# Up projections of two MLPs by one level of Strassen's method: seven quarter products per block

## The reference

```python
def sq_relu_mlp(h, w_up, w_down):
    return jnp.square(jax.nn.relu(h @ w_up)) @ w_down
```

## Time and profile before

| | us |
|---|---|
| median of three runs | 1588.3 (1588.07 to 1589.31) |
| the profiled execution, its own time | 1586.16 |
| its span in the profile | 1584.4 |
| first up unit of layer 0 starts | 500.8 |
| up 2 to up 15 with down 0 to 11, layer 0 | 526.5 to 887.0 |
| down 12 and 13, layer 0 | 887.0 to 914.2 |
| down 12 begins, layer 1 | 1513.4 |

### The profile page before, as it was taken

The page is one execution under the profiler, slowest core; times in us unless marked ns, Lnnn a source line. Parts: engine busy times, 40 slices in busy tenths (PEclk is TensorE's granted clock), DMA queues, the critical chain, the costliest instruction groups (busy, mean ns, idle before and its releaser), DMA issues.

```text
span 1584.4 us, 22657 instructions
## 1 busy us (share of the span) xinstructions
PE 1499.1 (95%) x9438; PEld 1334.8 (84%) x9438; DVE 865.4 (55%) x1298; ACT 502.2 (32%) x835; POOL 74.7 (5%) x119
## 2 busy tenths in 40 slices
PE   4899999988899999999999999989999999999995
PEld 3799999755688988998998879768899899889984
DVE  2693455677457644434334685935673433444378
ACT  2333333266516322222222244242632222222220
POOL 1200000010101000000000010000100000000002
PEclk8999999999999999999999999999999999999998
DMA  9421232475741322122222221461132222221211
GB/s 316 134 80 54 80 108 94 137 227 190 244 142 54 105 82 80 58 76 80 79 79 80 80 71 63 150 204 54 54 109 78 80 80 81 80 79 56 76 54 67
DMA packets 127770, 162.27 MB, mean 102 GB/s; under 512 B 3314, under 2 KB 103018, under 8 KB 127682
## 3 DMA queue, kind: packets, MB, share of 16 engines
q1 hardware_dynamic: 123106, 146.57, 28.6%
q0 software_dynamic: 3760, 11.80, 2.6%
q10 hardware_dynamic: 816, 2.65, 0.4%
HBM read 157.34 MB, written 3.67 MB: 102 GB/s over the span
## 4 chain that ended last, share of the span: by engine, by line
PE 86%; DVE 8%; ACT 2%; DMA 2%; issue 1%; POOL 0%; SPq 0%; ACTq 0%; DVEq 0%; POOLq 0%
PE ps L588 39%; PE ps L570 30%; PE ps L579 5%; PE ps L621 2%; PE ps L820 1%; PE ps L917 1%; DVE wlo L1544 1%; PE ps L797 1%; PE ps L940 1%; DMA raw<-in_w_mod_l 1%; PE ps L635 1%; DVE ln_small L1992 1%; PE ps L928 1%; ACT whi L1147 1%; DMA vec_rows<-in_b_mod_l 1%
## 5 line engine op out<-in xcount | busy, mean ns | idle before, releaser
L1147 ACT ACTIVATE whi<-raw 128x2048 fp32r<-128x2048 f32 x88 | 168.1, 1912 | 358.4 <-PE ps L588 353.4
L570 PE MATMUL ps<-h_hi,whi 128*128 128x320 f32 x1088 | 251.4, 313 | 12.3 <-DVE wlo L1544 7.7
L570 PE MATMUL ps<-h_lo,whi 128*128 128x320 f32 x1088 | 250.6, 312 | 0.0
L570 PE MATMUL ps<-h_hi,wlo 128*128 128x320 f32 x1088 | 250.3, 312 | 0.0
L588 PE MATMUL ps<-whi,hid_hi 128*128 128x512 f32 x640 | 249.4, 390 | 0.0
L588 PE MATMUL ps<-wlo,hid_hi 128*128 128x512 f32 x640 | 249.1, 389 | 0.0
L588 PE MATMUL ps<-whi,hid_lo 128*128 128x512 f32 x640 | 249.0, 389 | 0.0
L1544 DVE TENSOR_TENSOR wlo<-raw,whi 128x2048 fp32r<-128x2048 f32 x88 | 201.5, 2291 | 70.8 <-ACT whi L1147 66.7
L570 PEld LDWEIGHTS ps<-h_hi,whi 128*128 128x128 f32 x1088 | 184.7, 190 | 15.9 <-issue 11.8
L570 PEld LDWEIGHTS ps<-h_lo,whi 128*128 128x128 f32 x1088 | 184.4, 190 | 0.0
L570 PEld LDWEIGHTS ps<-h_hi,wlo 128*128 128x128 f32 x1088 | 184.4, 190 | 0.0
(11 more groups left out here) (269 smaller groups left out, 1871.8 us busy)
## 6 DMA issues: line engine op xcount, KB each, us to landing
raw<-in_w_mod_l SPq DMA_DIRECT2D x43, 1024.0 KB, 5.2
raw<-in_w_up_l SPq DMA_DIRECT2D x32, 1024.0 KB, 5.5
raw<-in_w_down_l SPq DMA_DIRECT2D x32, 1024.0 KB, 5.0
raw<-in_w_in_l SPq DMA_DIRECT2D x15, 1024.0 KB, 5.2
raw<-in_w_out_l SPq DMA_DIRECT2D x8, 1024.0 KB, 5.1
raw_more<-in_w_mod_l SPq DMA_DIRECT2D x5, 1024.0 KB, 9.8
out<-x_tok SPq DMA_DIRECT2D x5, 512.0 KB, 2.6
x_tok<-in_x_sample ACTq DMA_DIRECT2D x4, 512.0 KB, 6.8
```

The lines of the kernel that those rows point to most:

```text
L570: mm = pe.matmul(outs[hf], w_of(still, k), a_of(part, k, hf), start=(k == 0 and part == 0 and still == 0), stop=(k == nk - 1 and still == 1))
L1147: act.activation(whi[:, w % 2, :], raw_block(k), ACT.Copy).then_inc(hi_done, 1)
```

## The change

From up block 2 on, a block (1024 x 256 weights, 640 tokens) is cut into four weight quarters and four token quarters, and its product is made from seven quarter products of 12 matmuls each (Winograd's form), in place of eight. GpSimd forms the three weight sums that need it (`weight_sums`: four `tensor_tensor` instructions of 128 x 512; one sum is written over a raw quarter). The splits of a block become six pieces with seven quarters (3584 elements in place of 2048). VectorE forms the four sums of token quarters once per layer (`token_sums`), and puts seven products together with seven additions from PSUM (`combine`), two `squared` and two `low_u` in each block. The high and low parts of the token sums take the place of `x` (`thi` at the address of `x_tok`) and of unused quarters of `h`; the full-precision `h` (`hf32`) lies where `acc` is. So `x` is stored to memory by GpSimd's queue before the MLP (`spill_x`) and fetched back when up 15 has ended (`fetch_normed`), together with the norm's gain and bias; tiles 0 and 1 are then rescaled on VectorE, tiles 2 to 4 on GpSimd (`scale_x`), and all ten `gated_sum` come behind down 13. Down blocks are split in two pieces. The two gate vectors change places, and the mixer's gated output goes through the small buffer `pg`.

```diff
+        hf32 = at("h_full", 148, [P, KT, TOK])
+        thi = at("t_hi", 48, [P, KT, TOK], F32R)
+        tlo = at("t_lo", 176, [P, 2, 4, HALF], F32R)
+        sb = at("w_sums", 186, [P, 3, 512])
+        tf = tmp[:].rearrange("p a n -> p (a n)")
+        quad = [[tf[:, TOK * (1 + n):TOK * (2 + n)], tf[:, 0:TOK]] for n in range(2)]
...
+        NPROD, NCOMB = 7, 7
+        PAR = [w % 2 for w in W_UP]
+        PIECES = ((0,), (1, 2), (3,), (4,), (5,), (6,))
+        LN_X = (0, 2, 2 + NT, 4 + NT)
...
+            def spill_x(layer):
+                for t in range(NT):
+                    pool.wait_ge(ln_n, 2 * NT * layer + t + 1)
+                    pool.dma_start(A["x_spill"][t * P:(t + 1) * P, :], x[:, t, :]).then_inc(x_re, 16)
+            def weight_sums(layer, u, i=None):
...
+                r = raw_block(w_k[w]).rearrange("p (k n) -> p k n", n=BW)
+                a11, a12, a21, a22 = r[:, 0:4, 0:P], r[:, 4:8, 0:P], r[:, 0:4, P:BW], r[:, 4:8, P:BW]
+                s2, s1, s4 = (sb[:, n, :].rearrange("p (k n) -> p k n", n=P) for n in range(3))
+                raw_ready(pool, w_k[w], i)
+                if u > 2:
+                    before = w - 1 if strassen(w - 1) else w - 3
+                    pool.wait_ge(lo_done, lin(OPS[before] + 2, PER, i))
+                pool.tensor_tensor(s1, a21, a22, ALU.add).then_inc(sums, 1)
+                pool.wait_ge(sums, lin(c + 1, 16, i))
+                pool.tensor_tensor(s2, s1, a11, ALU.subtract).then_inc(sums, 1)
+                pool.tensor_tensor(a21, a11, a21, ALU.subtract).then_inc(sums, 1)
+                if u > 2:
+                    pool.wait_ge(lo_done, lin(OPS[before] + 5, PER, i))
+                pool.wait_ge(sums, lin(c + 2, 16, i))
+                pool.tensor_tensor(s4, a12, s2, ALU.subtract).then_inc(sums, 1)
+            def fetch_normed(layer):
+                pool.wait_ge(up_mm[layer], 4 + 14 * NPROD)
+                pool.wait_ge(x_re, 16 * NT * (2 * layer + 2))
+                for t in range(NT):
+                    pool.dma_start(x[:, t, :], A["x_spill"][t * P:(t + 1) * P, :]).then_inc(x_re, 16)
+                load_gb(2 * layer)
+            def scale_x(layer):
+                pool.wait_ge(x_re, 16 * NT * (2 * layer + 3))
+                pool.wait_ge(gb_ld, 32 * (2 * layer + 1))
+                for t in range(2, NT):
+                    pool.tensor_tensor(x[:, t, :], x[:, t, :], gb[:, 0, :], ALU.mult).then_inc(x_g, 1)
+                    pool.wait_ge(x_g, 6 * layer + 2 * t - 3)
+                    pool.tensor_tensor(x[:, t, :], x[:, t, :], gb[:, 1, :], ALU.add).then_inc(x_g, 1)
+                pool.wait_ge(x_g, 6 * layer + 6)
+            def mlp(layer):
+                spill_x(layer)
+                for n in (2, 3):
+                    weight_sums(layer, n)
+                for kind, n, i in mlp_steps(pool):
+                    if kind == "up" and n > 3:
+                        weight_sums(layer, n, i)
+                fetch_normed(layer)
+                scale_x(layer)
+                load_gb(2 * layer + 1)
...
+            T1, T2 = t_part(0, 0, tlo[:, 1]), t_part(4, 1, tlo[:, 0])
+            T3, T4 = t_part(0, 1, hhi[:, 0:4, HALF:TOK]), t_part(4, 0, hlo[:, 0:4, HALF:TOK])
+            PRODUCTS = ((0, h_part(0, 0)), (1, T2), (2, T1), (3, T3), (0, h_part(4, 0)), (1, h_part(4, 1)), (2, T4))
             def up(layer, u, i=None):
                 w = w_ord[S.index(("up", layer, u))]
+                c = NCOMB * (14 * layer + u - 2)
+                for item, (b, moving) in enumerate(PRODUCTS):
+                    for g, its in enumerate(PIECES):
+                        if item == its[0]:
+                            pe.wait_ge(lo_done, lin(OPS[w] + g + 1, PER, i))
+                    if u == 2 and item == 0:
+                        pe.wait_ge(relu_h0[layer], 4 * (layer + 1))
+                    seen = (c - 2, c - 1, c, None, None, c + 1, c + 2)[item]
+                    if seen is not None and (u > 2 or item >= 5):
+                        pe.wait_ge(comb, lin(seen, 4 * NCOMB, i))
+                    if item == 4:
+                        pe.wait_ge(first_out, lin(14 * layer + u - 1, 4, i))
+                    if u == 2 and item in (1, 2, 3, 6):
+                        pe.wait_ge(t_lo, 4 * layer + (1, 2, 3, 4)[(1, 2, 3, 6).index(item)])
+                    product(b, w, item, moving).then_inc(up_mm[layer], 1)
...
+            def high_t(layer, n, k0, hf):
+                if n == 0:
+                    act.wait_ge(x_re, 16 * NT * (2 * layer + 2))
+                act.wait_ge(t_sum, 4 * layer + (3, 3, 3, 4)[n])
+                cols = slice(hf * HALF, (hf + 1) * HALF)
+                act.activation(thi[:, k0:k0 + 4, cols], hf32[:, k0:k0 + 4, cols], ACT.Copy).then_inc(t_hi, 1)
+            def first_quad(layer, u, i=None):
+                act.wait_ge(up_mm[layer], lin(4 + NPROD * (u - 2) + 1, 4 * NPROD, i))
+                if u > 3:
+                    act.wait_ge(sq_lo[layer], lin(2 * u - 3, 8, i))
+                act.activation(quad[u % 2][0][:, 0:HALF], bank(0, 0, HALF), ACT.Copy).then_inc(first_out, 1)
...
             def mlp(layer):
                 for n, (f, hf) in enumerate(FIRST):
                     first_relu(layer, f, hf)
+                    if n == 3:
+                        high_t(layer, 0, 4, 1)
+                        high_t(layer, 1, 0, 0)
+                    if n == 4:
+                        high_t(layer, 2, 0, 1)
+                        high_t(layer, 3, 4, 0)
                     if n == 5:
-                        split_hi(W_UP[layer] + 2)
+                        split_hi(W_UP[layer] + 2, None, (0, 1, 2))
+                late = True
                 for kind, n, i in mlp_steps(act):
                     w = w_ord[S.index((kind, layer, n))]
+                    if kind == "down":
+                        split_hi(w + 1, i, (0, 1, 2) if strassen(w + 1) else None)
+                        late = True
+                        continue
+                    if late:
+                        split_hi(w, i, (3, 4, 5))
+                        late = False
+                    first_quad(layer, n, i)
+                    if strassen(w + 1):
+                        split_hi(w + 1, i, (0, 1, 2, 3, 4))
+                        high_u(layer, n, 0, i)
+                        split_hi(w + 1, i, (5,))
+                    else:
+                        split_hi(w + 1, i)
+                        high_u(layer, n, 0, i)
+                    high_u(layer, n, 1, i)
                 split_hi(w_ord[S.index(("down", layer, 15))])
...
-                mark(dve.tensor_tensor(acc[:, t, cols], acc[:, t, cols], gate[:, 1, int(t == LAT), cols], ALU.mult))
+                if t >= 2:
+                    dve.wait_ge(x_g, 6 * layer + 2 * t - 2)
+                else:
+                    dve.wait_ge(ln_x, LN_X[2 * layer] + t + 1)
+                mark(dve.tensor_tensor(acc[:, t, cols], acc[:, t, cols], gate[:, 0, int(t == LAT), cols], ALU.mult))
...
+            def token_sums(layer):
+                def quarter(k0, hf):
+                    return hf32[:, k0:k0 + 4, hf * HALF:(hf + 1) * HALF]
+                b11, b12, b21, b22 = quarter(0, 0), quarter(0, 1), quarter(4, 0), quarter(4, 1)
+                dve.wait_ge(ln_lo, NT * 2 * layer + NT)
+                dve.tensor_tensor(b11, b12, b11, ALU.subtract).then_inc(t_sum, 1)
+                dve.wait_ge(t_sum, 4 * layer + 1)
+                dve.tensor_tensor(b12, b22, b12, ALU.subtract).then_inc(t_sum, 1)
+                dve.wait_ge(t_sum, 4 * layer + 2)
+                dve.tensor_tensor(b22, b22, b11, ALU.subtract).then_inc(t_sum, 1)
+                dve.wait_ge(t_sum, 4 * layer + 3)
+                dve.tensor_tensor(b21, b21, b22, ALU.subtract).then_inc(t_sum, 1)
+            def low_t(layer, n, k0, hf, dst):
+                dve.wait_ge(t_hi, 4 * layer + n + 1)
+                if n == 2:
+                    dve.wait_ge(up_mm[layer], 4)
+                cols = slice(hf * HALF, (hf + 1) * HALF)
+                dve.tensor_tensor(dst, hf32[:, k0:k0 + 4, cols], thi[:, k0:k0 + 4, cols].bitcast(F32),
+                                  ALU.subtract).then_inc(t_lo, 1)
+            def combine(dst, a, b, layer, prods, seen, i):
+                dve.wait_ge(up_mm[layer], lin(prods, 4 * NPROD, i))
+                if seen:
+                    dve.wait_ge(comb, lin(seen, 4 * NCOMB, i))
+                dve.tensor_tensor(dst, a, bank(b, 0, HALF), ALU.add).then_inc(comb, 1)
...
+            def squared(dst, src):
+                return dve.scalar_tensor_tensor(dst, src, 0.0, src, ALU.max, ALU.mult)
+            def up_step(layer, u, i, late):
...
+                q11, q12 = (quad[u % 2][0][:, n * HALF:(n + 1) * HALF] for n in range(2))
+                q21, q22 = (quad[u % 2][1][:, n * HALF:(n + 1) * HALF] for n in range(2))
+                if late:
+                    split_lo(w, i, (3, 4, 5))
+                if two_ups:
```

(124 more changed lines are left out.)

163 lines of the change are left out of this document (80 added, 83 removed).

## The result

The changed kernel takes 1601.4 us (median; 1601.1 to 1602.2) where the kernel before, run beside it, takes 1588.5: ratio 1.0082, with a 95% interval of 1.0064 to 1.0099. It is 0.8% slower. I had forecast 1573.0 and a range of 1561 to 1600. The profiled execution took 1601.32 us, its span is 1598.9.

A forecast was written before the change was run, and what follows sets the result against it. The prediction took TensorE's matmul issue to bound the MLPs. Saved matmuls -49.3 us, waits at the ends +23.2, clock +4, starts +6.8 gave -15.3 us: 1573.0 us, range 1561 to 1600.

The forecast's parts named there:

- I let one of its 2.1 us instructions in first: End of an MLP, before down 14's split: one GpSimd instruction delays VectorE; TensorE loses 0.6 us in down 13.
- I add one of them, 1.1 us: Start of an MLP: GpSimd's weight sums meet crowded VectorE work, and one sum's 1.1 us is added.
- GpSimd blocks VectorE: Rival, both MLP ends and starts: GpSimd and VectorE instructions alternate; +7.5 us in all, 1595.8 us; chance 0.30.
- Steady state: Up and down block pairs: an up block takes 12.32 us in place of 14.08, VectorE's lag costs zero.
- the rival of the VectorE-bound pair: Up blocks: longer VectorE steps lose 1.5 us a pair, 21 us over 14 pairs, 1594 us; chance 0.10.
- Start without interference: Start of an MLP: VectorE's token sums and low parts make TensorE late by 2.3 us, before any GpSimd sum.
- End without interference: End of an MLP: TensorE 11.6 us late at down 15's split in each layer, plus 2 us of clock.
- The clock: After TensorE's stand at an MLP's end the granted clock must recover: 2 us a layer.
- GpSimd's prices: GpSimd's two-operand instructions, weight sums and rescales: 1.1 us for 512 elements, 2.1 us for 1024.
- U + 15: End of an MLP: the fetch of `x`, gain and bias lands 15 us after up 15 ends (U).
- the late trip through memory: Rival, end of an MLP: the fetch lands 20 us after up 15 ends, giving 1581 us; chance 0.08.

The follow-up runs named there:

- Run 1: The change with GpSimd's gain and bias for token tiles 2 to 4 cut to one column: 1580.0 us, 0.9945 of the kernel before.
- run 2: The change with only one element of each GpSimd weight sum formed, the rest left out: 1591.2 us, 1.0017 of the kernel before.
- run 5: The change with both GpSimd's rescale of tiles 2 to 4 and its weight sums made tiny: 1565.2 us, 0.9868 of the kernel before.
- run 6: The change with the stores of `x` issued between GpSimd's shares of the norm, not together: 1601.3 us, 1.0089 of the kernel before.
- run 3: The change with all rescales on VectorE, tiles 2 to 4 in a row behind down 13's groups: 1594.4 us, 1.0034 of the kernel before.
- run 9: The change with the end spread on VectorE, stores between norm shares, and `low_t` 2 and 3 ahead of the last two first lows: 1570.6 us, 0.9890.
- run 10: As run 9, and GpSimd waits with up 3's weight sums until the low parts of the token sums are done: 1571.3 us, 0.9894.
- run 11: Spread end, stores between norm shares; last two first lows behind up 2's fourth `combine`, up 3's sums behind up 2's fifth split: 1569.6 us, 0.9888.
- run 4: The change with the split of down 15 moved ahead of the ten gated sums: 1600.5 us, 1.0081 of the kernel before.
- run 7: The change with all rescales on VectorE, an earlier fetch, and gate and rescale spread between groups at the MLP's end: 1571.9 us, 0.9888.

## Why the prediction was wrong

**The step that failed** is, at the end of an MLP, "I let one of its 2.1 us instructions in first". I gave GpSimd one hold for the whole stretch; the trace shows five before the split of down 14 is done, 2.1 us each. From them came the second wait of TensorE, 9.4 and 9.2 us, for which the forecast had 0.6. Run 1 shortens GpSimd's instructions there and gives 21 us back. At the start it is the same step, "I add one of them, 1.1 us": the trace shows six between `h_lo` at 507.23 and the last first low at 533.14, 1.0 to 1.1 us each, 6.2 in all. The price of a hold was right at both places, their number was not. The change loses 7.6 and 7.0 us in its two layers, and runs 2 and 5, with the sums made tiny, 1.2 and 0.6. So the holds of the sums cost 6.4 us a layer there, with what they cost in clock. Forecast and result differ by 29.8 us in the span (-15.3 and +14.5): 17.7 are waits at the two ends, 6.0 their clock, 7.8 the starts, less 1.8 that lie ahead of the MLPs.

**The rival "GpSimd blocks VectorE" is what happened**, in its own numbers: it gave 17.9 us from the landing to the end of the split of down 14 (measured 17.75), 20.0 us late at the end (measured 20.35 of idle time), 6.4 for the whole start (measured 7.6 and 7.0), and the 3 us instructions and the second long wait in down 13. It gave 7.5 us more than before, where the spans differ by 14.5; of the missing 7, 6.0 are the clock term of the ends, sized at 2 us a layer and measured at 5.8 and 4.2; the starts add 1.8 and the waits at the ends some 0.8, and the stretches ahead of the two MLPs were 1.8 us shorter. The Trainium skill, "SBUF — State Buffer", section "Who interferes with whom", has it that a two-operand VectorE instruction and a GpSimd instruction that reads on-chip memory keep each other out for their whole length; this trace agrees (3.30 us in place of 1.23). I gave the rival 0.30, on the ground that no row of before showed GpSimd holding VectorE. The rows could not show it, since GpSimd's instructions there read one to four elements each; the absence of evidence was no evidence.

**Steady state**: right. 12.32 us an up block, no wait, 24.64 us gained in each layer; the rival of the VectorE-bound pair is out.

**Start without interference**: 2.3 us forecast, 1.2 measured in layer 0 and 0.6 in layer 1 (run 5). The stores of `x` are issued together; run 6 shows that this costs nothing.

**End without interference**: 11.6 us and 2 of clock forecast, 10.9 and 1.9 measured in layer 0, 10.9 and 3.0 in layer 1 (run 5). The fetch landed at U + 15.5 (U + 15 forecast), so the late trip through memory is out.

**The clock**: 2 us a layer forecast for the end, 5.8 and 4.2 measured in the change. In layer 0 one gap costs 1.9 to 2.2 us (runs 1, 3 and 5, though run 3's is 18.1 us long and the others' 10.9), and two gaps of 9 to 11 us cost 3.9 to 5.9 (the change, runs 2 and 6). The forecast had no clock term for the start, where a wait of 2.7 us came with 2.5 us of longer matmuls.

**GpSimd's prices**: 1.1 us forecast for 512 elements, 1.31 measured alone, 1.0 to 1.1 as the hold (2.21 less 1.23, 1.59 less 0.48); 2.1 for 1024, 2.07 measured as the hold. It is 305 us busy in place of my 230, mostly since its waits for VectorE count as busy. The Trainium skill, "GPSIMD Engine Reference", section "Elementwise — side-by-side cycle accounting", gave an estimate of 1.1 us for 512 elements and 2.25 for 1024. Both are for a whole instruction. The trace's 1.31 is 17% above the first. For 1024 no instruction ran alone; the last one (901.62) still ran 2.23 us after VectorE's split had ended at 902.62, within 1% of the second.

**What stays open**: how to win back the 7 us at each start. Runs 2 and 5 show that they come from the sums, runs 9 to 11 that no order tried brings them back, not what would; sums that read less, or none for up 2 and 3 alone, weren't tried. The start lasts the same, 374.5 us, in both layers of the change, though layer 0 has more of it as slow clock and layer 1 more as waiting; that VectorE's queue sets its end is argued from this, not shown. Why the first MLP began 6 to 7 us later in the profiled executions of runs 4 and 11 than in most others isn't settled either.

## What to carry to other kernels

Work handed to GpSimd is not taken off VectorE when both read on-chip memory with two operands, as here: price it as GpSimd's own length added to VectorE's queue, wherever the two meet in a stretch that VectorE bounds, and compare that with doing it on VectorE. Beside a matmul-bound stretch the same instructions were free: the up pairs stayed at 24.64 us. When a queue is late, spread its work into the gaps ahead of the deadlines (run 7: 9 us lost in place of 26) rather than reorder it behind them: a reordered queue only moves the wait (runs 4, 9, 10, 11).

## What the runs showed that I had not expected

- The alternation is strict: with both queues full, VectorE's 1.23 us and GpSimd's hold of 2.07 us become 3.3 us for either, for five of VectorE's instructions and six of GpSimd's in a row.
- VectorE instructions that read one operand from PSUM and one from on-chip memory were not held: four evacuations in 2.47 us beside the last 2.23 us of a GpSimd instruction.
- A VectorE cast with a single operand was stretched too: `h_hi` took 1.79 us at 509.36, beside a weight sum, and 0.69 at 487.35, with GpSimd idle.
- Short waits cost clock as well: behind the 2.73 us before 536.79 the granted clock was 0.66 and 24 matmuls took 1.8 us longer. What a gap costs did not follow from its length here: one of 18.1 us (run 3) cost 1.9 us, one of 10.9 (run 5) as much, and the same two gaps 5.8 us in the change and 3.9 in run 6.
